# Moving weight splits, norms and square sums between the steps where one sublayer of a decoder meets the next

## The reference

```python
def layer(x, p, lp, mix_fn):
    x = x + 0.5 * rmsnorm(swiglu(rmsnorm(x, lp['f1_pre']), lp['f1_in'], lp['f1_out']), lp['f1_post'])
    h = rmsnorm(x, lp['mix_pre'])
    gq, gk, gv, gg, la, sq, sk, sv = project(h, lp['w_in'], lp['gate_w'], lp['gate_b'])
    o_gla, o_sb, new_state = mix_fn(gq, gk, gv, la, sq, sk, sv)
    m = merge(o_gla, gg, o_sb, lp['gla_norm'], lp['sb_norm'], lp['w_out'], x.dtype)
    x = x + rmsnorm(m, lp['mix_post'])
    x = x + 0.5 * rmsnorm(swiglu(rmsnorm(x, lp['f2_pre']), lp['f2_in'], lp['f2_out']), lp['f2_post'])
    gate = jax.nn.sigmoid(rmsnorm(x, lp['ple_pre']) @ lp['ple_w_gate'])
    e = p.astype(x.dtype) @ lp['ple_w_up']
    x = x + rmsnorm(gate * e, lp['ple_post'])
    return x, new_state
```

## Time and profile before

| | us |
|---|---|
| runs: median (lowest to highest, 3 runs) | 1343.42 (1341.89 to 1346.29) |
| the profiled execution: its time | 1343.51 |
| its span in the profile | 1340.5 |
| mean granted TensorE clock | 0.961 |
| PE / DVE / ACT / POOL busy | 1259.3 / 599.3 / 430.9 / 94.9 |

### The profile page before, as it was taken

The page is one execution under the profiler, slowest core; times in us unless marked ns, Lnnn a source line. Parts: engine busy times, 40 slices in busy tenths (PEclk is TensorE's granted clock), DMA queues, the critical chain, the costliest instruction groups (busy, mean ns, idle before and its releaser), DMA issues.

```text
span 1340.5 us, 22655 instructions
## 1 busy us (share of the span) xinstructions
PE 1259.3 (94%) x9576; PEld 1195.9 (89%) x9576; DVE 599.3 (45%) x785; ACT 430.9 (32%) x555; POOL 94.9 (7%) x127
## 2 busy tenths in 40 slices
PE   6999999999998999999897789899999999999894
PEld 6999999999998999998574379899999999999793
DVE  5444322343325676552554233854331244433755
ACT  4322221222224333121553253532222222222543
POOL 6100000000010021110000001000000000002011
PEclk9999999999998999999888679999999999999897
DMA  5222223222231322221332013032222322223201
GB/s 194 95 76 81 70 95 117 70 88 82 65 105 49 95 64 65 65 99 49 127 126 63 31 49 124 6 103 84 86 71 94 122 68 94 71 74 107 95 1 67
DMA packets 40801, 110.12 MB, mean 82 GB/s; under 512 B 4962, under 2 KB 7026, under 8 KB 40610
## 3 DMA queue, kind: packets, MB, share of 16 engines
q1 hardware_dynamic: 38930, 103.13, 23.6%
q0 software_dynamic: 1232, 5.01, 1.1%
q10 hardware_dynamic: 576, 1.08, 0.2%
HBM read 103.57 MB, written 5.64 MB: 81 GB/s over the span
## 4 chain that ended last, share of the span: by engine, by line
PE 84%; DVE 8%; ACT 5%; issue 2%; DMA 1%; DVEq 0%; ACTq 0%; SPq 0%
PE PS L496 66%; PE PS L507 7%; DVE w_lo L1419 2%; PE PS L745 1%; ACT w_hi L1017 1%; PE PS L528 1%; DMA raw<-in_f_in 1%; PE PS L891 1%; PE PS L772 1%; DVE extra L1999 1%; DVE a_lo L1451 1%; PE PS L882 1%; PE PS L971 1%; DVE sum_sq L1463 0%; PE PS L802 0%
## 5 line engine op out<-in xcount | busy, mean ns | idle before, releaser
L496 PE MATMUL PS<-a_hi,w_hi 128*128 128x272 f32 x1712 | 359.9, 292 | 12.9 <-DVE w_lo L1591 7.7
L496 PE MATMUL PS<-a_lo,w_hi 128*128 128x272 f32 x1712 | 356.7, 290 | 0.0
L496 PE MATMUL PS<-a_hi,w_lo 128*128 128x272 f32 x1712 | 355.0, 289 | 0.0
L496 PEld LDWEIGHTS PS<-a_hi,w_hi 128*128 128x128 f32 x1712 | 270.7, 190 | 17.5 <-issue 12.2
L1419 DVE TENSOR_TENSOR w_lo<-raw,w_hi 128x2048 fp32r<-128x2048 f32 (+3 forms) x100 | 191.3, 1916 | 209.2 <-ACT w_hi L1017 209.2
L496 PEld LDWEIGHTS PS<-a_hi,w_lo 128*128 128x128 f32 x1712 | 271.3, 190 | 0.0
L496 PEld LDWEIGHTS PS<-a_lo,w_hi 128*128 128x128 f32 x1712 | 271.2, 190 | 0.0
L1017 ACT ACTIVATE w_hi<-raw 128x2048 fp32r<-128x2048 f32 (+3 forms) x100 | 158.1, 1584 | 68.6 <-PE PS L496 63.7
L496 PE MATMUL PS<-h_hi,w_hi 128*128 128x272 f32 x664 | 137.6, 289 | 0.0
L496 PE MATMUL PS<-h_lo,w_hi 128*128 128x272 f32 x664 | 137.4, 288 | 0.0
L496 PE MATMUL PS<-h_hi,w_lo 128*128 128x272 f32 x664 | 136.1, 286 | 0.0
(11 more groups left out here) (376 smaller groups left out, 1448.9 us busy)
## 6 DMA issues: line engine op xcount, KB each, us to landing
raw<-in_f_in SPq DMA_DIRECT2D x86, 512.0 KB, 4.3
raw<-in_f_out SPq DMA_DIRECT2D x32, 384.0 KB, 3.4
raw<-in_f_out SPq DMA_DIRECT2D x32, 320.0 KB, 3.1
raw<-in_w_rest SPq DMA_DIRECT2D x40, 256.0 KB, 2.9
k_pages<-in_cache_sb_k SPq DMA_DIRECT2D x16, 256.0 KB, 2.8
raw<-in_w_out SPq DMA_DIRECT2D x8, 512.0 KB, 4.6
raw<-in_ple_w_gate SPq DMA_DIRECT2D x8, 512.0 KB, 4.6
x<-in_x SPq DMA_DIRECT2D x8, 272.0 KB, 7.3
```

The lines of the kernel that those rows point to most:

```text
L496: last = mm(PS[0:width, 4 * quad + 2 * c + half, 0:HALF], wt[:, cols], act[:, k, half * HALF:(half + 1) * HALF], start=(k == 0 and n == 0) ...
```

## The change

Four things are moved; no arithmetic is added or taken away.

1. **Weight splits.** The blocks of the last three steps of each `down1` go to `a_hi`/`a_lo`, whose content is dead by then, so that the two regular slots are free earlier. A table `edge_splits` says which blocks are split in steps 4 to 7. For `f1` the last step splits `in` 2 (128 columns) and `rest` 0 (1024 columns), which before came after the edge; for `f2` it splits nothing. `out` 1 and 2 are split inside the merge loop (after norms 2 and 6) instead of in the steps of `out`, `f2_up0` 0 and 1 in the steps of `out`, and `gate` 1 and 2 inside edge 2, behind tile 4 of half 0 and tile 2 (ACT) or 4 (DVE) of half 1.
2. **Norms and copies in ACT's order.** The second half's norm stands behind tile 4 instead of tile 1 (edges 0 and 1), the copies of the embedding tiles behind tiles 1, 3, 5, 7 instead of 0, 2, 4, 6.
3. **Sums.** DVE's last two additions of squares of half 0 stand between the tiles of half 1, those of half 1 behind the first drain (`edge_rest`). PE's `pre_sum` of half 0 stands behind tile 2 of half 1 instead of tile 0, and that of half 1 inside the third product.
4. **The end.** The second half's gate logits and product stand between the first half's outputs.

The diff, cut to its core (ACT and DVE change their lists of splits in the same way):

```diff
         for name in ("f1_down1", "f2_down1"):
-            PLACED[W0[name] + KD - 1] = tuple(t_[:].rearrange("p k t -> p (k t)")[:, 0:1280] for t_ in (a_hi, a_lo))
-        for w in (W0["out"] + 3, W0["f2_up0"] + 2):
-            PLACED[w] = (h_flat[0][:, 8 * T:8 * T + SLOT], h_flat[1][:, 8 * T:8 * T + SLOT])
+            for n in range(3):
+                PLACED[W0[name] + 5 + n] = tuple(t_[:, 1280 * n:1280 * (n + 1)] for t_ in a_flat)
+        for w, tile in ((W0["out"] + 2, 8), (W0["out"] + 3, 4), (W0["f2_up0"] + 2, 8)):
+            PLACED[w] = tuple(t_[:, tile * T:tile * T + SLOT] for t_ in h_flat)
+        def edge_splits(last, after):
+            return {4: [(last, 5), (last, 6)], 5: [(last, 7), after[0]], 6: [after[1]], 7: after[2:]}
...
# PE, edge_first and edge_second
-                        if k == 0:
-                            if half:
-                                pre_sum(2 * b + 2, 0)
-                            elif sums:
-                                post_sum(2 * b + 1, 1)
-                pre_sum(2 * b + 2, 1)
+                        if half and k == 2:
+                            pre_sum(2 * b + 2, 0)
+                        elif sums and not half and k == 0:
+                            post_sum(2 * b + 1, 1)
...
+                        if half == 0 and k == (1 if tiles == 2 else 3):
+                            pre_sum(2 * b + 2, 1)
...
# ACT, edge
-                        if half == 0 and k == (0 if between else 1):
+                        if half == 0 and k == (0 if between else 4):
                             norm(j, 1)
...
# ACT, ffn
-                stage(last, KD, down1(j), end=KD - 2)
-                for c in (KD - 2, KD - 1):
+                stage(last, KD, down1(j), end=4)
+                for c in range(4, KD):
                     t, quad, use = ticket(Step(c), last)
+                    for nxt, c_ in edge_splits(last, after)[c]:
+                        split_edge(nxt, c_, t)
                     if c < KD - 1:
-                        split_edge(last, KD - 1, t)
                         down1(j)(Step(c), t, quad, use)
-                    else:
-                        for nxt, c_ in after:
-                            split_edge(nxt, c_, t)
...
-            ffn("f1", 0, (("in", 0), ("in", 1)))
+            ffn("f1", 0, [("in", 0), ("in", 1), ("in", 2), ("rest", 0)])
             edge(0, "mix_pre")
-            split_edge("in", 2, T0["in"])
-            split_edge("rest", 0, T0["in"])
...
# ACT, merge loop (DVE the same)
+                if i in (2, 6):
+                    split_edge("out", 1 if i == 2 else 2, T0["merge"])
...
# ACT, edge 2
-            def between(k):
-                if k % 2 == 0:
+            def between(half, k):
+                if half == 0 and k % 2:
                     e_tiles(k // 2)
-                if k == 1:
+                if half == 0 and k == 4:
                     split_edge("gate", 1, T0["f2_down1"] + KD)
+                if half and k == 2:
+                    split_edge("gate", 2, T0["embed"] + 3)
...
# DVE, edge
                     for k in range(KD):
-                        if k + 1 < KD:
-                            if k:
-                                dve.wait_ge(sig["x_ready"], 16 * b + 8 * half + k)
-                            edge_update(b, half, k + 1, post)
+                        if k > 1:
+                            dve.wait_ge(sig["x_ready"], 16 * b + 8 * half + k - 1)
+                        edge_update(b, half, k, post)
+                        if k > 2:
+                            edge_add(b, half, k - 2)
+                        elif half and k:
+                            edge_add(b, 0, KD - 3 + k)
                         edge_x(b, half, k)
...
# DVE, edge 2
+            def between(half, k):
+                if half == 0 and k == 4:
+                    split_edge("gate", 1)
+                if half and k == 4:
+                    split_edge("gate", 2)
...
# DVE, the end
+                    if half == 0 and k == 2:
+                        gate_logits_half(1)
+                    elif half == 0 and k == 4:
+                        gate_out_half(1)
```

More of the change, by code:

```diff
@@ L601, in body @@
                     open_ticket(t, quad, use)
-                    dense(quad, slot_pair(W0[name] + st.c), tiles, n_k, rhs, ready).then_inc(sig["psum_full"], 1)
+                    dense(quad, placed(name, st), tiles, n_k, rhs, ready).then_inc(sig["psum_full"], 1)
                 if not first:
                     body(Step(0), ready)
-                steps(pe, first or 1, end or n, body)
+                    first = 1
+                if end is None:
+                    steps(pe, first, n, body)
+                    return
+                steps(pe, first, loop, body)
+                for c in range(loop, end):
+                    body(Step(c))
             def first_up(ready):
@@ L661, in ffn @@
                 product(f"{name}_up1", GROUPS[1], 2, KD, A)
-                product(f"{name}_down1", KD, 1, GROUPS[1], H, h_tiles(first + GROUPS[0]), end=KD - 1)
+                product(f"{name}_down1", KD, 1, GROUPS[1], H, h_tiles(first + GROUPS[0]), loop=5, end=KD - 1)
                 edge_last(b, H, GROUPS[1], 1)
@@ L990, in _ @@
                 last.then_inc(sig["psum_full"], 1)
-            product("out", 4, 2, KD, A, a_tiles(2), end=3)
+            product("out", 4, 2, KD, A, a_tiles(2), loop=1, end=3)
             edge_last(1, A, KD, 2)
@@ L1094, in edge @@
                             norm(j + 1, 0)
-                        if between and half == 0:
-                            between(k)
+                        if between:
+                            between(half, k)
             def stage(name, n, body, first=0, end=None):
```

104 lines of the change are left out of this document (51 added, 53 removed).

## The result

| | before | after |
|---|---|---|
| runs: median (lowest to highest) | 1344.70 (1341.89 to 1346.29, 4) | 1332.53 (1331.25 to 1334.04, 4) |
| the profiled execution: time / span | 1343.51 / 1340.5 | 1331.34 / 1329.3 |
| mean granted clock | 0.961 | 0.960 |

What follows compares the result with a forecast made beforehand. It took TensorE, busy 94% of the span, as the bound, leaving its waits and low clock to gain: 5.4 - 2.2 + 3.6 + 2.4 + 3.8 = 13.0 us, so 1343.5 - 13.0 = 1330.5 us, range 1326.5 to 1337.5.

Steps and rivals of the forecast that it cites:

- Edge 0: First edge, 407 to 458 us: removed waits and low clock, less a new 0.6 us wait, gain 5.4 us.
- DVE is through them at about 411.6: First edge, last step: DVE finishes both remaining weight splits by then, so the 2.58 us wait on the squares goes.
- second stretch: First edge, 422 to 440 us at low clock: 1.6 us if it goes too, of which one half, 0.8, was counted.
- Clock at edge 1: Second edge, 823 to 884 us: idle 6.2 us less the 2.61 us chain, gain 3.6 us, clock at 1.00 in the trace.
- Merge: Loop of eight head norms: the split at step 2 delays step 3, 2.2 us lost; the one at step 6 costs nothing.
- Edge 2: Third edge, 1236 to 1294 us: gate's first product starts earlier despite a 6 us wait and ScalarE-DVE coupling, gain 2.4 us.
- The end: Last 20 us: second half's logits taken at 1320.1 instead of 1324.21, its first output at 1327.15, gain 3.8 us.
- Rival (1): All three edges: clock falls at every wait, giving 1333 us; inside the forecast's range, no chance of its own.
- Rival (4): All three edges at low clock make the kernel slower, needing 170 more matmuls at half rate; chance 0.04.
- rival (2): Splits meet transfers or each other at the first and third edges, gain only 6.3 us, 1337 us; chance 0.20.
- no wait of TensorE on the squares of the first half at any edge: Sign that the prediction is right: at all three edges TensorE never waits for the first half's squares.
- The granted clock over the second edge: Sign that the prediction is wrong: a granted clock under 0.9 there.

Runs made afterwards that it cites:

- x5: Changed kernel with only the `rest` 0 split taken out of the last `f1_down1` step and put behind the first edge; 1333.75 us, ratio 0.9921 to the kernel before.
- x9: Changed kernel with the moves of x3, x4 and x5 together; 1323.40 us, ratio 0.9853 to the kernel before.
- x8: Changed kernel plus 15 and 19 extra matmuls filling TensorE's waits before the first a_lo products of the first and second edges; 1329.05 us, ratio 0.9891.
- x4: Changed kernel with the two splits in the merge loop behind head norms 6 and 7 instead of 2 and 6; 1330.38 us, ratio 0.9901.
- x2: Changed kernel with only VectorE's split for the second gate product moved from tile 4 to tile 6 at the third edge; 1329.97 us, ratio 0.9902.
- x3: As x2, and the fourth embedding copy moved from behind tile 7 to behind tile 6; 1327.39 us, ratio 0.9866 to the kernel before.
- x11: Changed kernel with the second half's gate logits and output put back behind all eight first-half outputs; 1337.32 us, ratio 0.9954.
- x1: The changed kernel run once more, unchanged; 1331.46 us, ratio 0.9909 to the kernel before.

## Why the prediction was right

- **Edge 0** (5.4, got 4.2 beside the 0.5 it began ahead). "DVE is through them at about 411.6" was wrong by 1.8 us, counted from the start of the step: the block for `rest` 0 landed 3.8 us into it instead of 2, and 0.8 us of the 2.58 stayed. (The "0.4 us behind TensorE's half" is 0.6 by the prediction's own numbers.) A stretch at the half clock stayed with it; in x5 and x9 both are gone. The half that I took of the second stretch is one whole or none: 3.4 of loss became 1.7.
- **Clock at edge 1** (3.6, got 1.7). This step failed. I took the clock of 1.00 from one execution of the kernel before; the idle time went as foreseen and only the 2.61 stayed, but in every one of the 11 later profiles with that wait the clock fell, and with the wait filled it did not. It cost 2.9 us here (41.7 us against x8's 38.8). A second error hid part of it: the waits that went took 4.6 us with the slower restart behind each (2.1 up to the first a_lo product, and 41.3 us against x8's 38.8 behind it), not 3.6.
- The Trainium skill (TensorE: Matmul & The Clock Gate, section "HAM oscillation — how this bites in real kernels") tells of a kernel in which every wait for a transfer brings the half rate back. Its waits are longer than those of edges 0 and 1, so it doesn't say what 2 us do; here 2.61 us alone brought it back in 11 profiles, and 2.03 us alone in neither x5 nor x9.
- **Merge** (-2.2): right in size and mechanism, and x4 shows that it is the split at step 2 alone.
- **Edge 2** (2.4, got 2.2): right, with the wait of about 6 us, the coupling of the two engines and VectorE's idle 3.04 us in front of its split. x2 and x3 show that 4.85 us more were to be had.
- **The end** (3.8): right in the profile and in x11. On this chain the table load took 1.28 us (from 1314.21) and the square began at 1315.83, 0.34 us after its end, when VectorE's product was there; in the first half it began at 1307.04, right behind the load at 1305.75. The 2.66 us in the Trainium skill (ScalarE: Activation LUTs, section "What ACT_TABLE_LOAD costs") would again be too much.
- `out` (1.0), the time outside the span (1.0) and the 0.5 before the last step were not in the sum and made up for most of what edges 0 and 1 lacked: that this pair of profiles came so near to 13.0 is luck, since the first two are chance. Without the three, the parts give 9.7. By the medians x1 is again 12.1 us under the kernel before, so the size of the gain holds; where the 2 us beyond the parts come from, the profiles don't show.
- Rival (1) is what happened: the clock fell at all three edges, and its 1333 fits the median of 1332.5. Rival (4), 170 more matmuls at the half clock, is out; rival (2) was right that a split meets its transfer, at a fifth of its price.
- Of the signs, "no wait of TensorE on the squares of the first half at any edge" failed at edge 0 (0.80 us). The granted clock over the second edge was 0.94 over 53 us as in the earlier trace rows and 0.90 over the 33 us shown, at the bound of 0.9 that would have meant "wrong".

## What to carry to other kernels

Before moving a weight split ahead of a critical step, ask two things of it: when its block lands, and what the partner engine does between its half of the split and yours; the two halves at the same tile made VectorE stand for ScalarE's (3.04 us) and ScalarE for VectorE's next tile, and two tiles between them took 2.24 us off the wait (x2); better still is a place behind the work that the next product waits for. Where TensorE stands still for some 2 us between full stretches, shorten them, or fill them with matmuls into a bank that is about to be started afresh. Shortening alone is no sure cure: one wait of 2.03 us was free at edge 0, one of 2.61 us was not at edge 1. Judge a term of 1 or 2 us by the rows of its own place; medians of 6 runs here scatter by as much.
